# One convolution tap per channel group from TensorE to VectorE, six low parts of weights from VectorE to GpSimd

## The chip, the cores and the metric

The kernel runs on one core of a Trainium2 chip. The metric is the device time of one execution in microseconds; the value given is the median of the runs.

## What is computed

Two blocks of two layers each on a sequence of 256 tokens with 1024 features. The first layer of the first block is the one that matters here: a convolution mixer, then a layer norm, then a mixture of 16 experts, whose weights are the bulk of what is read from memory. The mixer, from the reference:

```python
def conv_mixer(x, w_in, a_dw, a_dw_b, a_ln_g, a_ln_b, b_dw, w_out):
    u = jnp.einsum("bsd,de->bse", x, w_in)
    a_val, a_gate, b_b, b_c, b_x = jnp.split(
        u, [D_A, 2 * D_A, 2 * D_A + D_B, 2 * D_A + 2 * D_B], axis=-1)
    a = a_val * jax.nn.sigmoid(a_gate)
    a = causal_depthwise_conv(a, a_dw) + a_dw_b
    a = jax.nn.silu(layer_norm(a, a_ln_g, a_ln_b))
    bb = b_b * causal_depthwise_conv(b_c * b_x, b_dw)
    return jnp.einsum("bse,ed->bsd", jnp.concatenate([a, bb], axis=-1), w_out)
```

## The kernel before

**Weights and their split.** All weights stream through slots of SBUF in a fixed order (`STREAM`, `LOAD_ORDER`), issued by SyncE in `sync_load`; a load waits until the earlier content of its slot is released (`released`), for a dense chunk when the low part of its fourth piece has been made. A dense chunk has 2048 columns, four pieces of 512. `even_w_in` (`ew_in`) has 10 chunks, pieces 0 to 39, and `even_w_out` (`ew_out`) 4 chunks, pieces 40 to 55. Each piece is multiplied in three products of two halves: ScalarE makes the high part `wh` (`scalar_split`, line 409), VectorE the low part `wl = w - wh` (`vector_split`, line 415), and in two other stages GpSimd makes the low parts of four pieces (`pool_split`, line 422). There are four places for parts, so piece p + 4 can be split when TensorE has used piece p (`w_used`). TensorE's three products are lines 444 to 446 (`three`). `low_made` names the semaphore that says a low part is there.

**The first mixer.** Each engine has its own hand-written order. `even_tensor` goes through chunks 1 to 9 of `ew_in` (`tensor_features`, 12 matmuls of 256 columns for each piece), then `ew_out` chunk 0, which multiplies `GT[0:2]`, the gated product of the short convolution, through its parts `early_gh` and `early_gl` (line 631). Then come the mean matmuls of the layer norm (line 1051), which need all four `ev_sum`, then the residual (line 1385), the next `ew_out` chunk, the variance (line 1060) and the rest.

**The 31 taps** act on four groups of 128 channels, each 256 tokens wide. The first `PE_TAPS` (9) of each group are matmuls with a diagonal matrix (line 1038), 36 in all, issued two behind each piece of chunks 3 to 6 and one behind each piece of chunk 7. ScalarE makes the diagonals (line 1100), six buffers in turn. Tap 9 is made by ScalarE (`ev_first_tap`, line 1094), and the other 21 per group by VectorE (`convolve`, line 1176), each adding to `acc`. A tap reads `aP` and `acc`, both in SBUF, and a column of weights. `steps` says how many taps VectorE makes behind each low part (4 where nothing is said, from chunk 3 on), and what else it does there: `value` (line 1167), `product` (1183), `convolve_b` (1190), `gate_b` (1197). What is left is made by `convolve(len(taps))` after the loop; then the four `ev_sum` (line 1219) add the matmuls' part from PSUM.

**ScalarE** goes in the same steps: the high part of the piece one chunk ahead, then up to two diagonals, then what else is due. **GpSimd** has one instruction in the mixer until its norm, the `pow` for the variance (line 1273).

Of the kernel before, what the change touches and what calls it, by code (L numbers as in the profile page):

```python
# [18 lines left out]
LN_EPS, RMS_EPS = 1e-5, 1e-6  # L19
RING, SMALL_RING, EXTRA = 12, 7, 12  # L20
PIECE, NPIECE = 512, 4
PE_TAPS = 9
MIXER_OUT = ("ew_out", "ow_out")
ROUTED = ("ew_out", "ow_out")
CH = 2048
# [21 lines left out]
CHUNK, KIND, PIECES, RUN_END = {}, [], {}, []  # L47
# [44 lines left out]
def f32(ap):  # L92
    return ap.bitcast(F32)
# [106 lines left out]
class Signals:  # L200
# [11 lines left out]
    def up(self, name, *step):  # L212
        shared = SHARED.get(name, name)
        steps = self.made.setdefault(shared, {})
        assert (name, *step) not in steps, (name, step)
        steps[(name, *step)] = len(steps) + 1
        return self.sem(shared), 1

    def at(self, name, *step):
        shared = SHARED.get(name, name)  # L220
        return self.sem(shared), self.known[shared][(name, *step)] if self.known else 1


class Kernel:
# [193 lines left out]
    def pool_split(self, p):  # L418

        pool = self.pool  # L420
        pool.wait_ge(self.at("w_hi", p))
        pool.e.tensor_tensor(self.wl[:, p % NPIECE, :], self.piece_source(p), f32(self.wh[:, p % NPIECE, :]),
                             ALU.subtract).then_inc(*self.up("w_lo_pool", p))

    def low_made(self, p):

        by_pool = any(0 <= p - PIECES[name] < NPIECE for name in ("ow_in", "aq0"))
        return self.at("w_lo_pool" if by_pool else "w_lo", p)

    def scalar_split_after(self, p):  # L430
# [1 line left out]
            self.scalar_split(p + NPIECE)  # L432

    def vector_split_after(self, p):
        if p + NPIECE < RUN_END[p]:
            self.vector_split(p + NPIECE)

    def weight(self, p):
# [573 lines left out]
    def even_tensor(self):  # L1012
        pe, at, up, PS, v = self.pe, self.at, self.up, self.PS, self.even_views()
        pe.wait_ge(at("consts", "ident"))
        for _ in range(7):
            pe.e.matmul(PS[:, 7, 0:128], self.ident[:, :], self.ident[:, :], start=True, stop=True)
        for q in range(4):
            pe.wait_ge(self.x_in[q // 2])
            for j in range(2):
                k = 2 * q + j  # L1020
                for h in range(2):
                    t = pe.e.transpose(PS[:, q, j * 256 + h * 128:j * 256 + h * 128 + 128],
                                       self.X[:, h, k * 128:k * 128 + 128], self.ident[:, :])
            t.then_inc(*up("turned", "ev", q))
            if q % 2:
                self.tensor_busy(7, 1)
        p, conv = PIECES["ew_in"], 0
        for c in range(10):
            if c == 0:
                self.tensor_opening_chunk("ev", p, 6)  # L1030
                continue
            if c >= 6:
                pe.wait_ge(self.even_bank_read((0, 1, 4, 5)[c - 6]))
            for _ in self.tensor_features("ev", p + 4 * c, (None, 1, 2, 3, 4, 5, 0, 1, 4, 5)[c]):
                for _ in range(0 if c < 3 or c > 7 else 1 if c == 7 else 2):
                    ch, k = conv // PE_TAPS, conv % PE_TAPS
                    pe.wait_ge(at("ev_dve", 1 + 2 * (ch // 2)), at("ev_diag", conv), at("ev_pad"))
                    pe.e.matmul(PS[:, 6 + ch // 2, ch % 2 * 256:ch % 2 * 256 + 256], v["dgs"][conv % 6],  # L1038
                                v["aP"][:, ch, k:k + 256], start=(k == 0), stop=(k == PE_TAPS - 1)).then_inc(
                        *up("ev_conv", conv))  # L1040
                    conv += 1
        assert conv == 4 * PE_TAPS
        p = PIECES["ew_out"]
        for c in (2, 3, 6, 7):
            pe.wait_ge(self.even_bank_read(c))
        for _ in self.tensor_out("ew_out", p, 8, 0):
            pass
        pe.wait_ge(at("consts", "mean"))
        for c in range(4):
            pe.wait_ge(at("ev_sum", 3))  # L1050
            t = pe.e.matmul(PS[:, 6, 0:256], self.mean512[:, :], v["acc"][:, c, :], start=(c == 0), stop=(c == 3))
        t.then_inc(*up("ev_mean"))
        for b in range(2):
            self.tensor_residual(b)
        for n in self.tensor_out("ew_out", p, 8, 1):
            if n == p + 4:
                pe.wait_ge(at("ev_square"))
                for h in range(2):
                    for c in range(4):
                        t = pe.e.matmul(PS[:, 7, h:h + 1], v["sq"][:, c, h * 128:h * 128 + 128], self.mean512[:, 0:1],  # L1060
                                        start=(c == 0), stop=(c == 3))
                t.then_inc(*up("ev_var"))
            if n == p + 5:
                pe.wait_ge(at("ev_rdiag", 1), at("consts", "ones"))
                for h in range(2):
                    t = pe.e.matmul(PS[:, 6, h * 128:h * 128 + 128], self.ones[:, 0:128], v["rs"][:, h * 128:h * 128 + 128],
                                    start=True, stop=True)
                t.then_inc(*up("ev_spread"))
        for b in range(2, 4):
            self.tensor_residual(b)  # L1070
        for _ in self.tensor_out("ew_out", p, 8, 2):
            pass
        self.tensor_out_last("ew_out", p, 8)

    def even_scalar(self):
# [11 lines left out]
        for c in range(10):  # L1087
            for j in range(4):
# [3 lines left out]
                for ch in {(2, 0): (0, 1), (4, 0): (2, 3)}.get((c, j), ()):  # L1092
                    act.wait_ge(at("ev_dve", 1 + 2 * (ch // 2)), at("ev_pad"))
                    act.e.activation(v["acc"][:, ch, :], v["aP"][:, ch, PE_TAPS:PE_TAPS + 256], ACT.Copy,
                                     scale=v["aw"][:, ch, PE_TAPS:PE_TAPS + 1]).then_inc(*up("ev_first_tap", ch))
                for _ in range(0 if c < 2 else 2 if diag < 4 * PE_TAPS - 1 else 4 * PE_TAPS - diag):
                    if diag >= 6:
# [171 lines left out]

    def even_pool(self):  # L1270
        pool, sm = self.pool, self.sm
        pool.wait_ge(self.at("var_eps", "ev"), self.at("consts", "mhalf"))
        pool.e.tensor_tensor(sm[:, 500:502], sm[:, 490:492], self.mhalf[:, 0:2], ALU.pow).then_inc(*self.up("rstd", "ev"))
        self.pool_norm("ew_out")
# [2062 lines left out]
```

## Time and profile before

| | us |
|---|---|
| median of 3 runs | 1743.29 |
| lowest, highest | 1742.96, 1743.67 |
| profiled execution | 1743.21 |
| its span | 1741.9 |
| TensorE busy | 1699.2 (98%) |
| VectorE busy | 793.8 (46%) |
| ScalarE busy | 623.6 (36%) |
| GpSimd busy | 126.0 (7%) |
| queue of the weight loads, share of the DMA engines | 77.2% |

The profiled execution lies 0.08 us under the median, and 1.3 us of it lie outside the span. The shares are averages over stages with different limits: in the two expert layers transfers and TensorE carry the time, in the dense stages TensorE with VectorE and ScalarE that make its operands. The granted TensorE clock is full (0.996 of 2.4 GHz). The first mixer takes the stretch from 0 to some 112 us; its convolution lies between 27 and 88 us.

### The profile page before, as it was taken

What the parts mean: (1) busy time and instruction counts of PE and PEld (TensorE: products, weight loads), DVE (VectorE), ACT (ScalarE), POOL (GpSimd) and SP (SyncE); (2) the same over time, 40 slices, a digit from 0 to 9 for tenths busy, and PEclk for the clock granted to TensorE, in tenths of its full rate; (3) what the DMA queues carried; (4) which work ended last, traced back from release to release, by engine and by line L of the source; (5) the groups of instructions that cost most, each with busy time, mean ns of one, the idle gap of its engine ahead of it and who ended that gap; (6) DMA issues with size and microseconds to landing.
All of it is one profiled execution on the core that took longest, in us unless ns stands there. A gap on an engine that the chain in (4) does not pass through costs nothing.

```text
span 1741.9 us, 23928 instructions
## 1 busy us (share of the span) xinstructions
PE 1699.2 (98%) x9970; PEld 1111.2 (64%) x9970; DVE 793.8 (46%) x1528; ACT 623.6 (36%) x1197; POOL 126.0 (7%) x150
## 2 busy tenths in 40 slices
PE   9999999998999999999999989999999999999998
PEld 9974334433234984344343333887999899789997
DVE  6961111111003791111111012866888677868885
ACT  6541100000003660100010002656666564756665
POOL 0000000000001000000000001231111011301101
PEclk9999999999899999999999999999999999999999
DMA  9869999999999799999999999534555544435550
GB/s 384 340 255 413 424 428 427 428 427 427 426 424 420 291 378 394 422 430 428 428 428 427 426 426 419 198 125 142 186 178 194 194 169 146 145 134 176 187 194 24
DMA packets 56948, 544.90 MB, mean 313 GB/s; under 512 B 6400, under 2 KB 6400, under 8 KB 8832
## 3 DMA queue, kind: packets, MB, share of 16 engines
q1 hardware_dynamic: 56416, 542.14, 77.2%
q8 instruction: 83, 1.36, 0.3%
q10 hardware_dynamic: 416, 1.13, 0.2%
q14 instruction: 33, 0.27, 0.0%
HBM read 542.19 MB, written 1.05 MB: 312 GB/s over the span
## 4 chain that ended last, share of the span: by engine, by line
PE 77%; DMA 17%; DVE 4%; issue 1%; ACT 1%; POOL 0%; ACTq 0%; SPq 0%; DVEq 0%
PE PS L1324 24%; DMA ring<-in_w 17%; PE PS L444 13%; PE PS L446 13%; PE PS L445 13%; PE PS L1306 2%; PE PS L1378 2%; PE PS L1524 2%; PE PS L1038 1%; PE PS L1340 1%; PE PS L2068 1%; PE PS L1392 1%; DVE wl L415 1%; PE PS L1497 1%; DVE sm L658 0%
## 5 line engine op out<-in xcount | busy, mean ns | idle before, releaser
L1324 PE MATMUL PS<-ring,F 128*64 128x512 f32 x1984 | 446.7, 598 | 23.7 <-DMA ring<-in_w 15.6
L415 DVE TENSOR_TENSOR wl<-ring,wh 128x512 fp32r<-128x512 f32 x496 | 359.4, 743 | 136.5 <-ACT wh L409 133.7
L409 ACT ACTIVATE wh<-ring 128x512 fp32r<-128x512 f32 x504 | 314.9, 630 | 266.5 <-PE PS L446 245.7
L1324 PEld LDWEIGHTS PS<-ring,F 128*64 128x64 f32 x1984 | 140.3, 137 | 306.8 <-issue 273.9
L444 PE MATMUL PS<-xh,wl 128*128 128x256 f32 x1120 | 322.3, 288 | 0.7 <-DVE wl L415 0.7
L445 PE MATMUL PS<-xl,wh 128*128 128x256 f32 x1120 | 316.8, 283 | 0.0
L446 PE MATMUL PS<-xh,wh 128*128 128x256 f32 x1120 | 316.8, 283 | 0.0
L444 PEld LDWEIGHTS PS<-xh,wl 128*128 128x128 f32 x1120 | 214.7, 192 | 3.7 <-DVE wl L415 2.0
L445 PEld LDWEIGHTS PS<-xl,wh 128*128 128x128 f32 x1120 | 214.8, 192 | 0.5
L446 PEld LDWEIGHTS PS<-xh,wh 128*128 128x128 f32 x1120 | 214.7, 192 | 0.0
L444 PE MATMUL PS<-wh,xl 128*128 128x512 f32 x320 | 129.7, 405 | 0.2 <-DVE F L2609 0.2
L1851 DVE COPY F<-PS 64x512 f32<-64x512 f32 x26 | 18.1, 695 | 223.1 <-PE PS L1324 223.1
L1826 DVE SCALAR_TENSOR_TENSOR F<-F,PS 128x512 f32<-128x512 f32 x28 | 19.3, 688 | 209.1 <-ACT F L1641 209.1
L446 PE MATMUL PS<-wh,xh 128*128 128x512 f32 x272 | 106.2, 391 | 0.0
L445 PE MATMUL PS<-wl,xh 128*128 128x512 f32 x272 | 106.1, 390 | 0.0
L1831 DVE SCALAR_TENSOR_TENSOR F<-F,PS 128x512 f32<-128x512 f32 x28 | 19.3, 688 | 172.7 <-PE PS L1324 172.7
L1324 PE MATMUL PS<-F 128*64 128x512 f32 x384 | 87.1, 593 | 0.0
L1641 ACT ACTIVATE F<-PS 128x512 f32<-128x512 f32 x28 | 16.7, 597 | 194.3 <-PE PS L1324 194.3
L1659 ACT ACTIVATE F<-PS 64x512 f32<-64x512 f32 x26 | 15.4, 591 | 187.6 <-PE PS L1324 187.6
L2801 DVE SCALAR_TENSOR_TENSOR F<-PS,cols,F 128x254 f32<-128x254 f32 (+1 forms) x176 | 76.4, 475 | 1.6
L1324 PE MATMUL PS<-early,F 128*64 128x512 f32 x336 | 76.1, 594 | 0.0
L1649 ACT ACTIVATE F<-PS 128x512 f32<-128x512 f32 x28 | 16.6, 595 | 152.5 <-PE PS L1392 152.5
(453 smaller groups left out, 2048.2 us busy)
## 6 DMA issues: line engine op xcount, KB each, us to landing
ring<-in_w SPq DMA_DIRECT2D x98, 2048.0 KB, 25.3
ring<-in_w SPq DMA_DIRECT2D x68, 1024.0 KB, 11.1
ring<-in_ffn_up SPq DMA_DIRECT2D x44, 1024.0 KB, 4.9
early<-in_w SPq DMA_DIRECT2D x16, 2048.0 KB, 26.2
F<-in_w SPq DMA_DIRECT2D x15, 2048.0 KB, 26.1
F<-in_w SPq DMA_DIRECT2D x22, 1024.0 KB, 10.5
ring<-in_ffn_down SPq DMA_DIRECT2D x22, 1024.0 KB, 4.9
ZX<-in_w SPq DMA_DIRECT2D x7, 2048.0 KB, 26.3
```

The lines of the kernel that those rows point to most:

```text
L409: act.e.activation(self.wh[:, p % NPIECE, :], self.piece_source(p), ACT.Copy).then_inc(*self.up("w_hi", p))
L415: dve.e.tensor_tensor(self.wl[:, p % NPIECE, :], self.piece_source(p), f32(self.wh[:, p % NPIECE, :]), ALU.subtract).then_inc(*self.up("w_ ...
L444: e.matmul(out, left[1], right[0], start=first, stop=False)
L445: e.matmul(out, left[0], right[1], start=False, stop=False)
L446: return e.matmul(out, left[0], right[0], start=False, stop=last)
L1306: t = pe.e.matmul(self.PS[:, 6 + half, k4 * 128:k4 * 128 + 128], self.X[:, h, k * 128:k * 128 + 128], v["S"][:, h, :], start=(h == 0), sto ...
L1324: t = pe.e.matmul(PS[64 * half:64 * half + 64, bank, :], lhs(k), weights[:, a:a + 512], start=(k == 0), stop=(k == 7))
L1378: t = pe.e.matmul(self.PS[:, b, :], v["Gt"][:, h, d, :], v["Y"][d], start=(q == 0), stop=False)
L1524: t = pe.e.matmul(PS[64 * half:64 * half + 64, self.first_bank(ex, 0), :], xg[:, k, ex * 64:ex * 64 + 64], weights[:, a:a + 512], start=(k ...
L1826: e.scalar_tensor_tensor(out=self.silu(ex), in0=self.silu(ex), scalar=1.0, in1=PS[:, 4, :], op0=ALU.add, op1=ALU.mult).then_inc(*up("silu" ...
L1831: e.scalar_tensor_tensor(out=v["hh"], in0=self.silu(ex), scalar=0.5, in1=PS[:, 5, :], op0=ALU.mult, op1=ALU.mult).then_inc(*up("hidden", l ...
L2801: t = dve.e.scalar_tensor_tensor(out=dst[:, j, s:256], in0=ps[:, j, 0:256 - s], scalar=cw[:, k, 2 - s:3 - s], in1=dst[:, j, s:256], op0=AL ...
```

## The change

`PE_TAPS` becomes 8. TensorE makes 32 conv matmuls, two behind each piece of chunks 3 to 6 and none in chunk 7. ScalarE makes 32 diagonals and tap 8 as the first one; VectorE makes taps 9 to 30, 22 per group, 88 in all instead of 84. The numbers in `steps` are as they were.

The low parts of the last piece of chunks 3 to 8 (pieces 15, 19, 23, 27, 31 and 35, `SHARED_LOWS`) are made by GpSimd, at the head of its part of the mixer. Each of these waits for its high part and for VectorE's low part of the piece before, so that the release of the slot, which follows this fourth low part, still says that all four were read. `low_made` sends TensorE's and SyncE's waits for these pieces to GpSimd's semaphore.

```diff
-PE_TAPS = 9
+PE_TAPS = 8
@@ pool_split
         pool.wait_ge(self.at("w_hi", p))
+        if p in self.SHARED_LOWS:
+            pool.wait_ge(self.at("w_lo", p - 1))
         pool.e.tensor_tensor(self.wl[:, p % NPIECE, :], self.piece_source(p), f32(self.wh[:, p % NPIECE, :]),
                              ALU.subtract).then_inc(*self.up("w_lo_pool", p))

+    SHARED_LOWS = [PIECES["ew_in"] + 4 * c + 3 for c in range(3, 9)]
+
     def low_made(self, p):
-        by_pool = any(0 <= p - PIECES[name] < NPIECE for name in ("ow_in", "aq0"))
+        by_pool = p in self.SHARED_LOWS or any(0 <= p - PIECES[name] < NPIECE for name in ("ow_in", "aq0"))
@@ vector_split_after
-        if p + NPIECE < RUN_END[p]:
+        if p + NPIECE < RUN_END[p] and p + NPIECE not in self.SHARED_LOWS:
             self.vector_split(p + NPIECE)
@@ even_tensor
-                for _ in range(0 if c < 3 or c > 7 else 1 if c == 7 else 2):
+                for _ in range(0 if c < 3 or c > 6 else 2):
@@ even_pool
         pool, sm = self.pool, self.sm
+        for p in self.SHARED_LOWS:
+            self.pool_split(p)
```

## Rows read from the trace of the kernel before

**Rows 1.** Busy time by stretches: stretch, its length, busy us by engine, clock, DMA

```profile
50.00:60.00 10.00, 10.00 (x73) 9.56 (x72) 9.97 (x23) 5.74 (x13) 0.00 (x0) 1.00 1.01 424
60.00:70.00 10.00, 10.00 (x75) 9.62 (x74) 9.98 (x24) 5.02 (x10) 0.00 (x0) 1.00 1.03 424
70.00:80.00 10.00, 10.00 (x84) 9.95 (x83) 10.00 (x21) 5.28 (x10) 0.00 (x0) 1.00 0.58 215
120.00:130.00 10.00, 9.61 (x56) 6.03 (x55) 3.40 (x21) 2.21 (x6) 0.00 (x0) 1.00 0.57 200
```

**Rows 2.** Chain that ended last, first mixer: start, length, what

```profile
70.20 0.43 PE PS L1038 x2
...
82.15 0.24 issue
82.39 0.47 PE PS L444
82.86 0.23 PE PS L445
...
88.11 1.73 PE PS L1051 x8
```

**Rows 3.** Timeline of VectorE, first mixer: start, length, line, instruction

```profile
44.21 1.67 DVE L1176 SCALAR_TENSOR_TENSOR F<-F,cols 128x256 f32<-128x256 f32 x4
45.89 0.69 DVE L415 TENSOR_TENSOR wl<-ring,wh 128x512 fp32r<-128x512 f32 x1
...
48.66 0.69 DVE L415 TENSOR_TENSOR wl<-ring,wh 128x512 fp32r<-128x512 f32 x1 [0.49 <-ACT wh L409]
...
53.64 1.67 DVE L1176 SCALAR_TENSOR_TENSOR F<-F,cols 128x256 f32<-128x256 f32 x4
55.22 0.69 DVE L415 TENSOR_TENSOR wl<-ring,wh 128x512 fp32r<-128x512 f32 x1
55.82 0.88 DVE L1176 SCALAR_TENSOR_TENSOR F<-F,cols 128x256 f32<-128x256 f32 x2
...
57.32 0.69 DVE L415 TENSOR_TENSOR wl<-ring,wh 128x512 fp32r<-128x512 f32 x1
...
59.61 0.69 DVE L415 TENSOR_TENSOR wl<-ring,wh 128x512 fp32r<-128x512 f32 x1
...
61.90 0.69 DVE L415 TENSOR_TENSOR wl<-ring,wh 128x512 fp32r<-128x512 f32 x1
...
81.41 0.70 DVE L631 TENSOR_TENSOR early_gl<-F,early_gh 128x512 fp32r<-128x512 f32 x1
...
85.00 0.89 DVE L1176 SCALAR_TENSOR_TENSOR F<-F,cols 128x256 f32<-128x256 f32 x2
85.79 1.66 DVE L1219 SCALAR_TENSOR_TENSOR F<-F,sm,PS 128x256 f32<-128x256 f32 x4
```

**Rows 4.** Timeline of ScalarE, high parts of pieces 28, 29 and 30

```profile
56.68 0.61 ACT L409 ACTIVATE wh<-ring 128x512 fp32r<-128x512 f32 x1
58.22 0.83 ACT L1100 ACTIVATE F<-ident,cols 128x128 f32<-128x128 f32 x2 [0.93 <-PE PS L1038]
58.96 0.62 ACT L409 ACTIVATE wh<-ring 128x512 fp32r<-128x512 f32 x1
...
61.25 0.61 ACT L409 ACTIVATE wh<-ring 128x512 fp32r<-128x512 f32 x1
```

**Rows 5.** Timelines of GpSimd and VectorE in a later dense stage, side by side

```profile
1223.85 1.61 POOL L2845 TENSOR_TENSOR F<-F 128x512 f32<-128x512 f32 x1
...
1234.66 1.29 POOL L2845 TENSOR_TENSOR F<-F 128x512 f32<-128x512 f32 x1
...
1234.77 1.73 DVE L415 TENSOR_TENSOR wl<-ring,wh 128x512 fp32r<-128x512 f32 x1 [0.68 <-ACT wh L409]
```

**Rows 6.** Timelines of GpSimd and VectorE after the first expert layer

```profile
550.43 1.28 POOL L422 TENSOR_TENSOR wl<-ring,wh 128x512 fp32r<-128x512 f32 x1 [435.79 <-ACT wh L409]
...
550.24 2.00 DVE L658 BATCH_NORM_STATS2 sm<-PS 128x6 f32<-128x512 f32 x3
```

## The prediction

> **What bounds the kernel now.** I read the busy time by stretches first. From 50 to 80 us both TensorE and VectorE are full (10.00 and 9.97 to 10.00 of 10), and the DMA share falls from 1.03 to 0.58: the weight slots are filled and the transfers wait for slots [rows 1]. So the first mixer is a compute stage, and what it ends late by moves the expert layer behind it; after 120 us the transfers start again with the slots that the experts give back (share 0.57 from 120 to 130, most of it idle time) [rows 1]. Second, the chain of waits: through the stretch it is TensorE alone, one matmul behind the other. It breaks once, at 82.15, where the first `ew_out` matmul waits for a low part of `GT` that VectorE ended at 82.11; that matmul ends at 82.86, while its followers end 0.23 apart [rows 2]. The mean matmuls (`ev_mean`) take 88.11 to 89.84, and TensorE has no gap before them [rows 2]. They need the last `ev_sum`. Third, VectorE's own timeline: the four `ev_sum` instructions start at 85.79 and last 1.66, so they end at 87.45, only 0.66 us before TensorE reaches them [rows 3]. Both engines are nearly critical at the point where they meet. The question is which of them the change helps, and the views to answer it are the timelines of VectorE and ScalarE and the rows where GpSimd and VectorE already run together.
>
> **TensorE.** Four conv matmuls of 36 go, one per channel group: all four single ones of chunk 7. The chain has such a single one at 0.43 [rows 2]; the four save 4 x 0.43 = 1.72 us, between 64 and 71 us. TensorE would stand before the mean at 88.11 - 1.72 = 86.4 if nothing else held it. ScalarE loses four `ev_diag` instructions (two take 0.83 [rows 4]) that no one waits for; its splits of pieces 29 and 30 no longer stand behind the diagonals, and come sooner.
>
> **VectorE, without contention.** It gains four taps. `convolve` takes a fixed number per step, so all four land in the last `convolve(len(taps))`, straight before the sums: two taps there now last from 85.00 to 85.79 [rows 3], so one costs 0.395 and four cost 1.58. It loses the low parts of pieces 15, 19, 23, 27, 31 and 35 (one is 0.60 from start to next start: 55.22 to 55.82 [rows 3]). Three of them save nothing: up to piece 24 VectorE waits for ScalarE (0.49 before 48.66, the low part of piece 24, and 0.1 a step before that: four taps and the low part after them are 1.68 apart at 44.21 and 45.89, where undelayed ones are 1.58 apart at 53.64 and 55.22 [rows 3]), and TensorE's and so ScalarE's pace is unchanged there. Piece 27 saves nothing either: piece 28's low part starts at 57.32, when its high part lands (56.68 + 0.61 = 57.29 [rows 3, 4]). What pays is 31 and 35: 2 x 0.60 = 1.20, and two waits of 0.10 for ScalarE, at 59.61 and 61.90, each right behind a high part (58.96 + 0.62, 61.25 + 0.61 [rows 3, 4]), where ScalarE will be earlier. Sum: +1.58 - 1.20 - 0.20 = +0.18: the sums end at 87.45 + 0.18 = 87.63, after TensorE's 86.4 and its earlier low part of `GT`. So even in the kind case the 1.72 us of TensorE is spent waiting for the sums. The mean starts at 87.7 from a standstill; a restart costs 0.25 to 0.5 (the first matmul after the gap at 82.15 took 0.24 + 0.47 where 0.23 is the pace [rows 2]), so the mean ends at 87.7 + 0.3 + 1.73 = 89.7 against 89.84. Gain: 0.1 us.
>
> **GpSimd.** Six subtracts are added. GpSimd has the same instruction on the same shape in later stages: 1.28 us [rows 6]. It is idle in this stretch, and TensorE wants each result about two pieces later. The tightest is piece 35: TensorE runs chunks 8 and 9 from 70.63 to 82.15, 1.44 a piece [rows 2], so it wants piece 35 at 70.63 + 3 x 1.44 - 1.72 = 73.2. Piece 34's low part, by the lag worked out below, ends near 71.3 and GpSimd's near 72.6. Nothing is late there. Its wait for the low part of p - 1 only keeps the slot release honest; SP, which issues the weight loads in order, gets the slots of these six chunks up to 0.6 later (1.28 - 0.69), and the loads behind one wait with it; while transfers queue anyway (share 1.01 and more to 70 us [rows 1]) and the slots are full before the experts start, that costs nothing; without that cover it would be 0.6.
>
> But the two engines disturb each other. A VectorE low part that starts at 1234.77 takes 1.73 instead of 0.69 while GpSimd's two-input TENSOR_TENSOR (1234.66, 1.29) runs: it ends 0.55 after GpSimd does [rows 5]. The loss is 1.04 us for 1.18 us of overlap: VectorE practically stands still. GpSimd in turn takes 1.61 instead of 1.29 when VectorE was there first [rows 5]. Instructions that read PSUM are spared: three statistics of PSUM beside the very subtract that is moved here take 2.00 us, 0.67 each, no more than the 0.69 of one undisturbed VectorE instruction over 512 elements (the low part at 55.22) [rows 3, 6]. In the mixer nearly all VectorE work reads two SBUF operands: low parts (`ring`, `wh`) and taps (`aP`, `acc`). No row shows a tap beside GpSimd. Its cost is bounded by zero (as the PSUM readers) and by GpSimd's whole 1.28; I take the low part's behaviour as nearest, 1.04 plus a little because VectorE is back to back here and never begins 0.11 late: 1.15 a piece. So each moved low part saves 0.60 and costs 1.15: +0.55, not -0.60. The Trainium skill, "SBUF — State Buffer", section "Who interferes with whom", states the general form: a VectorE instruction with two SBUF inputs and a GpSimd one that reads SBUF exclude each other for the whole instruction, whatever the operation. By it the taps are held like the low parts, and each piece costs the full 1.28, which adds 0.4 us to the sum below.
>
> **The sum.** VectorE's lag against before: pieces 15 to 23 cost 0.55 each, and VectorE has 0.8 us of waiting a chunk to take that in (three steps of 0.1 and the 0.49 [rows 3]): 0. Piece 27: +0.55 less the 0.1 that it waits before 57.32: +0.45. The waits at 59.61 and 61.90: -0.20. Pieces 31 and 35: +1.10. So the low part of `GT` comes at 82.11 + 1.35 = 83.46 and `ew_out` starts 1.35 late, though TensorE was 1.72 early. The four taps: +1.58. The last sum ends at 87.45 + 2.93 = 90.38. TensorE, ready at 88.11 + 1.35 = 89.46, waits 0.9; the mean ends at 90.38 + 0.3 + 1.73 = 92.4, 2.6 us later than 89.84. Behind it TensorE is the chain again and everything moves by the same 2.6 us; the experts' first slots are released by TensorE, so the stream restarts 2.6 later too. Span 1741.9 + 2.6 = 1744.5; the profiled execution's time 1743.21 + 2.6 = 1745.8; it lies 0.08 under the median of the runs, 1743.29, so the median becomes 1745.9. That is +0.15%. A measurement of this kernel can tell 0.2%, which is 3.5 us, from no change; this stays inside.
>
> **Rivals.** (A) GpSimd doesn't hold the taps, because a SCALAR_TENSOR_TENSOR is spared: then the sum without contention holds, -0.1: 1743.2. For: not all that VectorE does is held [rows 6], and no row has a tap beside GpSimd. Against: [rows 5], with two SBUF operands as the taps have. (B) The exclusion is dearer: each subtract first waits for the running VectorE instruction, is stretched to 1.61 as in [rows 5], and VectorE stands for all of it. Then a piece costs 1.61 - 0.60 = 1.01; 27, 31 and 35 give 0.91 + 2.02 - 0.20 = 2.73, with the taps 4.31, and some 0.3 that pieces 15 to 23 no longer hide; the mean ends 4.3 us late: 1747.6, slower by 0.25%. It decides when a piece costs more than about 1.45. Against: in [rows 5] the stretch came from a wait during which VectorE worked, so it is not lost twice. (C) TensorE's saving survives whole, since VectorE catches up: -1.7, 1741.6. It would need VectorE's sums 1.0 us earlier than now, and no row gives it that. (D) The loss is taken in behind the mixer, by a transfer wait that ends last: 1743.3. Against: slots are full before 120 us [rows 1], and no transfer is awaited there.
>
> **Chances.** Forecast 0.68; A 0.12, B 0.14, C 0.02, D 0.04. Own range of the forecast, from 1.04 to 1.28 a piece and restart 0.25 to 0.5: 1745.3 to 1746.7. For 8 in 10, with A or B partly: 1742.9 to 1747.3. Faster by over 0.2% would need 3.5 us, twice what TensorE sheds: 0.01. Slower by over 0.2%: B and a sliver of the forecast, 0.15. Within: 0.84.
>
> **What would show it.** Taps or low parts of 1.4 to 1.7 us at pieces 15 to 35, each ending just behind a GpSimd subtract; conv matmuls gone after 64.5; the last taps ending near 88.8 and the sums near 90.4; TensorE idle up to 1 us before the mean, naming VectorE's sum. If taps stay at 0.5 (0.89 less 0.395) beside GpSimd, A is right. If TensorE has no gap before the mean, my account of the last taps is wrong. If the mean comes 2.6 late and the span doesn't, D.

## The result, and the profile after

The changed kernel takes 1745.53 us (median of 22 runs, 1743.94 to 1748.35) against 1743.16 for the kernel before (22 runs, 1742.46 to 1745.30) beside it. The ratio is 1.0015, with a 95% interval of 1.0009 to 1.0021: slower by 2.4 us, and by less than the 0.2% taken as the bound of no change. The profiled execution took 1745.91, its span 1744.7.

The busy time of the changed kernel by stretches (columns as in [rows 1]) shows VectorE full from 60 to 90 us, while TensorE is not from 70 us on. Before, it was the other way round from 80 to 90 us: TensorE 9.76 of 10, VectorE 9.38.

```profile
60.00:70.00 10.00, 10.00 (x80) 9.72 (x79) 10.00 (x22) 4.91 (x9) 4.24 (x1) 1.00 1.01 419
70.00:80.00 10.00, 9.66 (x80) 9.35 (x79) 10.00 (x20) 4.52 (x9) 1.41 (x1) 1.00 0.53 202
80.00:90.00 10.00, 7.16 (x36) 5.69 (x35) 10.00 (x22) 4.80 (x8) 0.00 (x0) 1.00 0.69 255
```

The chain of the changed kernel, where [rows 2] had TensorE with one break of 0.24 us, runs through VectorE's taps, low parts and sums into the mean matmuls:

```profile
65.31 0.60 DVE wl L415
65.91 2.23 DVE F L1180 x3
...
83.46 0.86 DVE F L1180 x2
84.33 0.60 DVE wl L415
84.93 0.60 DVE F L1201
...
87.91 1.58 DVE F L1223 x4
89.49 0.14 issue
89.62 1.96 PE PS L1055 x8
```

The reader is to see the 2.23 for three taps, which otherwise take 1.19, and at the end that the mean matmuls (line 1055) wait for the sums (line 1223) and then take 1.96 instead of 1.73. The view of waits of TensorE from 60 to 100 us names the low part of `GT`, the sums and once, for 0.3 us, a low part of VectorE. It never names GpSimd, and from 20 to 60 us TensorE has no wait, so no low part that moved came too late for it:

```profile
PE PS L448 <- DVE early_gl L635: 1.7, 1, 1.7
PE PS L1055 <- DVE F L1223: 1.1, 1, 1.1
PE PS L448 <- DVE wl L415: 0.3, 1, 0.3
```

GpSimd's timeline in the mixer has the six added subtracts, for pieces 15, 19, 23, 27, 31 and 35:

```profile
27.08 1.32 POOL L424 TENSOR_TENSOR wl<-ring,wh 128x512 fp32r<-128x512 f32 x1 [22.48 <-ACT wh L409]
36.53 2.18 POOL L424 TENSOR_TENSOR wl<-ring,wh 128x512 fp32r<-128x512 f32 x1 [8.13 <-ACT wh L409]
45.69 1.47 POOL L424 TENSOR_TENSOR wl<-ring,wh 128x512 fp32r<-128x512 f32 x1 [6.98 <-ACT wh L409]
54.83 2.17 POOL L424 TENSOR_TENSOR wl<-ring,wh 128x512 fp32r<-128x512 f32 x1 [7.68 <-ACT wh L409]
62.83 4.24 POOL L424 TENSOR_TENSOR wl<-ring,wh 128x512 fp32r<-128x512 f32 x1 [5.83 <-ACT wh L409]
70.68 1.41 POOL L424 TENSOR_TENSOR wl<-ring,wh 128x512 fp32r<-128x512 f32 x1 [3.61 <-DVE wl L415]
```

VectorE's timeline beside them, as [rows 3]:

```profile
27.18 2.29 DVE L1180 SCALAR_TENSOR_TENSOR F<-F,cols 128x256 f32<-128x256 f32 x3
...
43.96 4.27 DVE L1180 SCALAR_TENSOR_TENSOR F<-F,cols 128x256 f32<-128x256 f32 x8
...
53.39 2.45 DVE L1180 SCALAR_TENSOR_TENSOR F<-F,cols 128x256 f32<-128x256 f32 x6
55.76 0.68 DVE L1187 TENSOR_TENSOR F<-F,PS 128x512 f32<-128x512 f32 x1
57.08 0.69 DVE L415 TENSOR_TENSOR wl<-ring,wh 128x512 fp32r<-128x512 f32 x1 [0.64 <-ACT wh L409]
...
65.83 2.31 DVE L1180 SCALAR_TENSOR_TENSOR F<-F,cols 128x256 f32<-128x256 f32 x3
...
70.46 2.70 DVE L1180 SCALAR_TENSOR_TENSOR F<-F,cols 128x256 f32<-128x256 f32 x4
...
85.46 2.45 DVE L1180 SCALAR_TENSOR_TENSOR F<-F,cols 128x256 f32<-128x256 f32 x6
87.84 1.64 DVE L1223 SCALAR_TENSOR_TENSOR F<-F,sm,PS 128x256 f32<-128x256 f32 x4
```

Four taps without a neighbour last 1.66 from the first's start to the last's end, three 1.27. The groups at 27.18, 43.96, 65.83 and 70.46 are each longer by 1.02 to 1.04. The six taps at 53.39 are not, though GpSimd's subtract starts at 54.83 in their midst; it takes 2.17 instead of 1.28, so it waits for about 0.9 us, until VectorE comes to `product`, which reads PSUM (55.76). Piece 19's subtract does the same with `value`, which reads PSUM too: 36.53 + 2.18 - 1.28 = 37.43, and `value` starts at 37.46.

**One mark for all traces.** The first conv matmuls come between 27.3 and 28.7 us in the traces here, whatever the kernel; so I lay the traces on the start of the first pair of conv matmuls and count from there. In TensorE's timeline of the kernel before it is

```profile
27.86 1.02 PE L1038 MATMUL PS<-F 128*128 128x256 f32 x4
```

and in the changed kernel's

```profile
27.61 1.02 PE L1042 MATMUL PS<-F 128*128 128x256 f32 x4
```

From this mark, in us. "Sums" are the four `ev_sum` instructions; the names in the first column are those of the runs in the next section; the last column runs from the first matmul of the first expert (line 1524 in the kernel before) to GpSimd's first low part behind that expert layer (an expectation below calls it the stretch from the first gather):

| kernel | sums end | against before | mean matmuls end | against before | length of the first expert layer |
|---|---|---|---|---|---|
| before | 59.59 | | 61.98 | | 425.65 |
| changed | 61.87 | +2.28 | 63.97 | +1.99 | 426.64 |
| changed, again | 61.85 | +2.26 | 63.97 | +1.99 | 425.51 |
| taps_only | 60.97 | +1.38 | 63.09 | +1.11 | 426.58 |
| lows_only | 60.51 | +0.92 | 62.88 | +0.90 | 426.10 |
| extra_subtract | 63.45 | +3.86 | 65.79 | +3.81 | 425.37 |
| extra_memset | 59.59 | 0.00 | 61.98 | 0.00 | 425.73 |
| late_two | 61.85 | +2.26 | 63.96 | +1.98 | 425.69 |
| two_free_lows | 60.98 | +1.39 | 63.08 | +1.10 | 425.13 |
| balanced | 59.40 | -0.19 | 61.52 | -0.46 | 426.50 |
| balanced_nine | 58.83 | -0.76 | 61.56 | -0.42 | 425.37 |
| nudge_short | 61.85 | +2.26 | 63.97 | +1.99 | 425.42 |
| nudge_long | 61.86 | +2.27 | 63.98 | +2.00 | 425.84 |

The mixer's columns repeat to 0.02 us between executions (the two traces of the changed kernel); the last column doesn't. So the mixer is read from the traces, and the run times only confirm it.

### The profile page after: what moved, and what is told of

Same layout as the page of the kernel before. It is cut to its first block, busy times and chain, and to the rows that moved or that the text cites. A ratio compares the mean times of both kernels' runs of the same rounds, so it can differ in the third digit from the quotient of the medians.

```text
span 1744.7 us, 23918 instructions
## 1 busy us (share of the span) xinstructions
PE 1696.0 (97%) x9962; PEld 1109.3 (64%) x9962; DVE 795.4 (46%) x1526; ACT 622.1 (36%) x1193; POOL 138.9 (8%) x156
## 4 chain that ended last, share of the span: by engine, by line
PE 75%; DMA 18%; DVE 5%; issue 1%; ACT 1%; POOL 0%; ACTq 0%; SPq 0%; DVEq 0%
PE PS L1330 23%; DMA ring<-in_w 17%; PE PS L448 13%; PE PS L450 12%; PE PS L449 12%; PE PS L1312 2%; PE PS L1384 2%; PE PS L1530 2%; DMA ring<-in_a_w_in 1%; DVE wl L415 1%; DVE F L1180 1%; PE PS L2074 1%; PE PS L1042 1%; PE PS L1398 1%; PE PS L1503 1%
## 5 line engine op out<-in xcount | busy, mean ns | idle before, releaser
L415 DVE TENSOR_TENSOR wl<-ring,wh 128x512 fp32r<-128x512 f32 x490 | 354.9, 742 | 137.6 <-ACT wh L409 135.1
```

Of the source, the lines that this page charges most:

```text
L415: dve.e.tensor_tensor(self.wl[:, p % NPIECE, :], self.piece_source(p), f32(self.wh[:, p % NPIECE, :]), ALU.subtract).then_inc(*self.up("w_ ...
```

## The experiments

**Each half of the change alone.** The taps:

```diff
-    SHARED_LOWS = [PIECES["ew_in"] + 4 * c + 3 for c in range(3, 9)]
+    SHARED_LOWS = []
```

> The changed kernel with all low parts of the mixer back on VectorE: only the move of one tap per channel group is left. My theory (VectorE sets the end of the convolution, and the four taps land straight before its sums): VectorE's sums end 1.58 - 0.20 = 1.4 us later than before (88.8), TensorE stands idle before the mean matmuls about 0.9 us, their end comes at 90.9 instead of 89.84, and the time rises by 1.1 us. Rival (TensorE sets it, its four matmuls less pay): the mean matmuls end 1.7 us earlier and the time falls by 1.7 us.

Measured: the sums 1.38 later, the mean matmuls 1.11; TensorE's wait before them is 1.1 us. The time is 1744.70 against 1743.37 (ratio 1.0009, 1.0000 to 1.0018). VectorE's timeline and the chain of this kernel:

```profile
84.73 2.46 DVE L1180 SCALAR_TENSOR_TENSOR F<-F,cols 128x256 f32<-128x256 f32 x6
87.11 1.64 DVE L1223 SCALAR_TENSOR_TENSOR F<-F,sm,PS 128x256 f32<-128x256 f32 x4
...
88.77 0.14 issue
88.90 1.97 PE PS L1055 x8
```

Six taps stand before the sums where [rows 3] had two. TensorE's four matmuls less bring nothing: the rival, 1.7 us earlier, falls.

The low parts, on the changed kernel:

```diff
-PE_TAPS = 8
+PE_TAPS = 9
@@ even_tensor
-                for _ in range(0 if c < 3 or c > 6 else 2):
+                for _ in range(0 if c < 3 or c > 7 else 1 if c == 7 else 2):
```

> The kernel before with the six low parts on GpSimd and nothing else changed. My theory (a GpSimd subtract stops VectorE's instructions with two SBUF operands for 1.04 us, more than the 0.60 that the moved low part saves, and only pieces 31 and 35 count, since VectorE waits for ScalarE up to piece 28): VectorE's sums and the mean matmuls come 2 x 0.44 = 0.9 us later, the time rises by 0.9 us; up to 1.3 if piece 27 counts too. Rival (no exclusion): VectorE's sums come 1.2 us earlier, TensorE is the bound as before, the wait of 0.24 to 0.5 us at the start of the output product goes, and the time falls by 0.2 to 0.5 us.

Measured: sums +0.92, mean matmuls +0.90, time 1744.73 against 1743.37 (1.0007, 0.9998 to 1.0016). Taking six low parts of 0.60 off VectorE makes it later. The rival, a gain, falls. The two halves add up to the whole: 1.38 + 0.92 = 2.30 for the sums, where the changed kernel has 2.28. But TensorE meets the delay at another place here: it has no wait before the mean matmuls and one of 1.1 us (0.2 in the kernel before) at the low part of `GT`, which ends 0.91 later.

**What excludes what.** The kernel before with GpSimd work that no one needs:

```diff
@@ even_pool, on the kernel before
+        free = self.F[:, 6272:6528]
+        wide = [free.bitcast(mybir.dt.bfloat16).rearrange("p (a b) -> p a b", a=2)] + [x.unsqueeze(1).to_broadcast([128, 2, 256]) for x in (self.cmask[:, :], self.ones[:, :])]
+        for p in [PIECES["ew_in"] + 4 * c + 3 for c in range(3, 9)]:
+            pool.wait_ge(self.at("consts", "cmask"), self.at("w_hi", p), self.at("w_lo", p - 1))
+            pool.e.tensor_tensor(wide[0], wide[1], wide[2], ALU.subtract).then_inc(*self.up("consts", "extra", p))
+            pool.wait_ge(self.at("consts", "extra", p))
```

> The kernel before, with six GpSimd subtracts added beside it at the same six places (they read two idle tiles of 512 elements a partition and write a third; no one waits for them); VectorE keeps all its low parts and TensorE its 36 taps. My theory (exclusion, about 1.04 us for each that meets two-operand VectorE work): pieces 31 and 35 cost 2.1, 27 up to 0.9, and each of the first three leaves up to 0.3 that the waits for ScalarE don't take in: VectorE's sums and the time come 2.1 to 3.5 us later. Rival (the two engines run side by side freely): no difference, since nothing waits for these instructions.

Measured: sums +3.86, time 1747.07 against 1743.37 (1.0024, 1.0014 to 1.0034). VectorE's timeline at pieces 27 and 31:

```profile
54.98 2.69 DVE L1176 SCALAR_TENSOR_TENSOR F<-F,cols 128x256 f32<-128x256 f32 x4
...
64.55 2.69 DVE L1176 SCALAR_TENSOR_TENSOR F<-F,cols 128x256 f32<-128x256 f32 x4
```

The direction and the price of one are as expected (2.69 is 1.03 over 1.66), the sum is 0.4 above the range. Piece 28's low part already starts 2.0 us late, counted from the mark (31.47 against 29.46); two waits of 0.1 take 0.2 of it, and pieces 31 and 35 add 2.07. I had let the waits for ScalarE take in too much of the first four. One of them is piece 27, whose subtract met taps here, and not an instruction that reads PSUM (2.69 at 54.98).

```diff
@@ in place of the subtract
+            for i in range(4):
+                pool.e.memset(free, 0.0).then_inc(*self.up("consts", "extra", p, i))
+                pool.wait_ge(self.at("consts", "extra", p, i))
```

> As the run with the added subtracts, but each is replaced by four GpSimd memsets of 256 elements (about 1.2 us together) that read nothing. My theory (what excludes is the reading of SBUF): VectorE's instructions keep 0.48 and 0.69 us beside them, the mean matmuls end where they did, the time stays within 0.3 us. Rival (any GpSimd work on SBUF stops VectorE): the same loss as with the subtracts, 2.1 us or more.

Measured: sums and mean matmuls to the hundredth where they were; 1743.16 against 1743.37 (1.0001, 0.9992 to 1.0011). GpSimd's and VectorE's timelines at piece 31:

```profile
63.05 1.42 POOL L1276 MEMSET F<- 128x256 f32 x4 [6.77 <-ACT wh L409]
...
62.26 1.67 DVE L1176 SCALAR_TENSOR_TENSOR F<-F,cols 128x256 f32<-128x256 f32 x4
```

The same time of GpSimd work, writing only, leaves the taps at 1.67. GpSimd's writing is thereby ruled out as what stops VectorE, and its reading is what is left. The memsets differ from the subtract in more than that: they are another operation, and four short instructions in place of a long one. No run separates these. This is how the Trainium skill has it ("SBUF — State Buffer", "Who interferes with whom"): a VectorE instruction with two SBUF inputs contends with a GpSimd instruction that reads SBUF and not with one that only writes.

**Which of the six count.** Two kernels, with the changed kernel's list cut:

```diff
-    SHARED_LOWS = [PIECES["ew_in"] + 4 * c + 3 for c in range(3, 9)]
+    SHARED_LOWS = [PIECES["ew_in"] + 4 * c + 3 for c in (7, 8)]
```

> The changed kernel with only pieces 31 and 35 on GpSimd; 15, 19, 23 and 27 go back to VectorE. My theory (the first four cost and save nothing, since VectorE waits for ScalarE up to piece 28 in either case): VectorE's sums and the mean matmuls stand where they stand in the changed kernel, 2.3 and 2.0 us behind the kernel before when both traces are laid on their first conv matmul; the time within 0.3 us of the changed kernel's. Rival (each of the six costs the same): a third of the loss from GpSimd, 2 x 0.44 of the sums' 2.3, has to be spread over six, and the sums come 0.6 us earlier than in the changed kernel.

```diff
+    SHARED_LOWS = [PIECES["ew_in"] + 4 * c + 3 for c in (4, 6)]
```

> The changed kernel with only pieces 19 and 27 on GpSimd, the two whose subtract gets its turn beside a VectorE instruction that reads PSUM. My theory: no VectorE instruction is stretched, the sums and the mean stand as with the taps alone (1.38 and 1.1 us behind the kernel before on the same mark), for VectorE gives the time that it saves back as a wait for ScalarE. Rival (exclusion costs at any place): 0.9 us more than that.

Measured: with 31 and 35 alone the sums stand at +2.26, as with all six; with 19 and 27 alone at +1.39, as with none. Both as expected. The times are 1744.32 against 1743.05 (1.0007, 0.9998 to 1.0016) and, one run, 1743.02, where the mixer's +1.1 drowns in the scatter.

**The taps elsewhere.** `balanced` is the changed kernel with all low parts on VectorE, `balanced_nine` the kernel before; in both, `steps` becomes (shortened):

```diff
-                 (2, 3): [(convolve, 2)], (3, 3): [(convolve, 2), (value, 1)], ...
-                 (7, 0): [(convolve, 3)], (7, 1): [(convolve, 3)], (7, 2): [(convolve, 3)],
+                 (2, 3): [(convolve, 4)], (4, 1): [(convolve, 5)], (4, 3): [(convolve, 5)], (3, 3): [(convolve, 2), (value, 1)], ...
+                 (7, 0): [(convolve, 2)], (7, 1): [(convolve, 2)], (7, 2): [(convolve, 2)],
```

> PE_TAPS 8, all low parts on VectorE, and the taps' places changed: two more behind piece 15's low part and one more each behind those of 21 and 23, where VectorE waits for ScalarE, and one less behind each of 32, 33 and 34, so three fewer stand before the low part of GT. My theory: the sums end 1.38 - 4 x 0.395 = 0.2 us earlier than before, the low part of GT 1.4 us earlier, so output product 1.4 us earlier; the mean matmuls end at the sums' 87.25 + 0.14 + 1.96 = 89.35, 0.5 us earlier than before; the time falls by 0.5 us, too little to be told by the time alone. Rival (TensorE's four matmuls are what counts once VectorE is not in the way): 1.7 us.

> The kernel before (PE_TAPS 9, nothing on GpSimd) with the taps' places changed in the same way. My theory: VectorE's sums come 1.6 us earlier, but TensorE is then the one that ends last; only its wait for the low part of GT goes, and the mean matmuls end 0.5 us earlier (0.24 + 0.24); the time falls by 0.5 us. Rival (VectorE alone sets the end in the kernel before too): 1.6 us earlier.

Measured, `balanced`: sums -0.19, mean matmuls -0.46, as expected (-0.2, -0.5), so its rival, 1.7 us earlier, falls; 1742.53 against 1743.05 (0.9998, 0.9989 to 1.0007). `balanced_nine`: mean matmuls -0.42 as expected, but the sums only -0.76 instead of -1.6; 1742.92 against 1743.05 (1.0001, 0.9992 to 1.0010). VectorE's timeline of `balanced_nine` shows why, at pieces 35 and 36:

```profile
71.21 0.69 DVE L415 TENSOR_TENSOR wl<-ring,wh 128x512 fp32r<-128x512 f32 x1 [0.36 <-ACT wh L409]
...
73.14 0.69 DVE L415 TENSOR_TENSOR wl<-ring,wh 128x512 fp32r<-128x512 f32 x1 [0.24 <-ACT wh L409]
```

VectorE, freed of three taps just before, waits for ScalarE again, which follows TensorE, and TensorE still has its four matmuls in chunk 7. Piece 35's low part should have come 1.19 earlier (three taps) and comes 0.74 earlier, piece 36's 0.40 earlier: these two waits cost the missing 0.8. Both versions put the mixer some 0.45 us ahead of the kernel before; neither beats it by a time that can be told.

**How GpSimd gets in.** Piece 31's subtract took 4.24 us, of which 1.28 are its own; `late_two` gave 4.24 once more, `lows_only` 1.30. I took it for a matter of phase and shifted the request by a memset of 16 or 160 elements:

```diff
@@ pool_split, on late_two
             pool.wait_ge(self.at("w_lo", p - 1))
+            pool.e.memset(self.F[:, 6272:6288], 0.0).then_inc(*self.up("consts", "nudge", p))
+            pool.wait_ge(self.at("consts", "nudge", p))
```

> The changed kernel with only pieces 31 and 35 on GpSimd, and a memset of 16 elements before each of the two subtracts, which shifts them by about 0.15 us. My theory (when GpSimd asks for the port against back-to-back VectorE work, the phase decides whether it is let in at once or waits for many instructions; VectorE loses its 1.04 us once in either case): piece 31's subtract takes 1.3 to 1.5 us instead of 4.24, and the sums stay where they are, 2.3 us behind the kernel before. Rival (a kind of VectorE instruction or the piece decides): 4.24 again.

> The same with memsets of 160 elements, a shift of about 0.3 us. My theory: the phase decides again, so that one of the two subtracts may wait long (over 2 us) or both be let in at once; the sums again 2.3 us behind the kernel before, within 0.3. Rival (the piece decides): 4.24 for piece 31 and 1.4 for piece 35 again.

GpSimd's timelines, the short shift first:

```profile
63.70 4.07 POOL L426 TENSOR_TENSOR wl<-ring,wh 128x512 fp32r<-128x512 f32 x1
...
71.54 1.64 POOL L426 TENSOR_TENSOR wl<-ring,wh 128x512 fp32r<-128x512 f32 x1
```

```profile
63.28 3.95 POOL L426 TENSOR_TENSOR wl<-ring,wh 128x512 fp32r<-128x512 f32 x1
...
71.12 1.52 POOL L426 TENSOR_TENSOR wl<-ring,wh 128x512 fp32r<-128x512 f32 x1
```

The theory of the phase falls: the subtract starts later and ends at the same place in VectorE's sequence, behind piece 32's low part, so 4.24 becomes 4.07 and 3.95. Counted from the mark it ends between 39.45 and 39.47 in the changed kernel's two traces, `late_two`, `nudge_short` and `nudge_long`. The sums didn't move. The piece alone doesn't decide either, for `lows_only` has 1.30 at piece 31. What lets GpSimd in stays open.

**The changed kernel again.**

> The changed kernel again, for a second trace of it. My theory (the mixer's loss is fixed by the orders of the engines, and what its first trace showed beyond it, 1.0 us more in the first expert layer, is that execution's own): on the mark of the first conv matmul the sums come 2.3 and the mean matmuls' end 2.0 us after those of the kernel before, and the stretch from the first gather to the end of the first expert layer is anywhere between 425.1 and 426.6 us. Rival (the change makes the first expert layer slower too): that stretch is again 426.6 or more.

Measured: sums +2.26 and mean matmuls +1.99, and 425.5 us for the expert layer where the first trace had 426.6. The time is 1745.35 against 1743.62 (1.0010, 1.0001 to 1.0019). The extra 1.0 us in the first trace was that execution's own: over all thirteen traces this stretch lies between 425.1 and 426.6 without regard to the mixer.

## Why the prediction was right, point by point

- **What bounds.** Right: VectorE's last sum sets the mean matmuls (TensorE waits 1.1 us for it, 0.9 forecast), and the 1.72 us that TensorE sheds go nowhere. `taps_only` puts the sums at +1.38, which is 1.58 - 0.20 to the hundredth.
- **Where the four taps land.** Right: six taps last 2.45 before the sums at 87.84, where two did in [rows 3].
- **The price of a moved low part.** The mechanism was right, taps are held like low parts (rival A falls with `lows_only` and with the 2.31 and 2.70 above). The size was a little off: 1.04 for each, exactly the loss in [rows 5], not 1.15. VectorE's back-to-back work does not make it dearer, and 1.28, the price for a hold over GpSimd's whole instruction, was too high as well. So +0.44 a piece instead of +0.55. B (1.61 lost) falls too: GpSimd's own time grows to 4.24, yet VectorE loses 1.04.
- **Which pieces count.** One term was wrong: piece 27 was put at +0.45 and costs nothing. Its subtract got in with `product`, which reads PSUM, and ended in VectorE's wait of 0.64 before 57.08; in `extra_subtract`, where the same piece met taps, they took 2.69 in place of 1.66. I had not looked at what VectorE would be doing when GpSimd is let in.
- **The sum.** Forecast +2.93 for the sums, measured +2.28. The difference is piece 27's 0.45 and 2 x 0.11 for the price: 2.26 is left, which is what `late_two` and the second trace of the changed kernel show. The same two terms explain the low part of `GT`: +1.35 forecast, +0.67 measured (54.92 against 54.25 from the mark). The mean matmuls: +2.6 forecast, +2.0 measured. So the mechanism came as forecast, and the delay was put 0.6 us too long.
- **The restart.** 0.3 was forecast over 1.73; measured are 0.14 of issue and 1.96, together 0.37.
- **GpSimd's results.** "Nothing is late there" held for TensorE, but not for the reason given: piece 31's low part was there 2.5 us later than VectorE's used to be (39.46 against 36.93 from the mark), where up to 0.6 was reckoned. Its slot is released by so much later too; the DMA share from 60 to 70 us stays at 1.01 (1.03 before).
- **Behind the mixer.** The first matmul of the first expert comes at 96.92 from the mark in the kernel before and 98.93 in the changed one, +2.01: the loss is handed on whole, D falls. The loads move with it: the group issued at 126.75 in the kernel before is issued at 128.51 in the changed one, +2.01 from the mark. One reading was wrong and did no harm: the transfers don't start again after 120 us; in the kernel before their share is 1.01 from 110 to 120 already. That the median (1745.53, +2.4) came as near to the forecast (1745.9, +2.6) as it did owes something to luck: the traces support +2.0, which over 1743.16 is 1745.2, just under the forecast's own range (1745.3 to 1746.7), and the repeated comparison gave +1.7.
- **C** falls with `taps_only`: TensorE's saving doesn't survive.

## What to carry to other kernels

Before work goes from VectorE to GpSimd, look in the trace for a place where both run: if VectorE's instruction reads two operands from SBUF and GpSimd's reads two as well, the stretched instruction gives the price of the move. Here it was 1.04 us for each subtract of 1.28, against 0.60 saved, so the move lost 0.44 wherever VectorE had no wait to take it in. Where GpSimd got in beside a VectorE instruction that reads PSUM (pieces 19 and 27), the move cost nothing; it gained nothing either, because VectorE waited for ScalarE there. Work taken from one of two engines that meet gains nothing if the other has no slack (1.72 us off TensorE gave nothing here), and with hand-written orders where the work lands matters as much as its amount: here added taps fell straight before the result that all wait for, while the waits they could have filled lay 30 us and more before.

## What the runs showed of the hardware that I had not expected

- GpSimd can wait for its turn through many VectorE instructions. In the changed kernel its subtract for piece 31 starts at 62.83 and, by its own 1.28, was let in near 65.8 (an estimate): it waited through six taps of the long and the short convolution and a low part, back to back. In `lows_only`, at the same point of the taps (0.76 us after the group's start, against 0.77), it was let in at once. The shifts of 0.2 and 0.3 us did not change the place. VectorE loses its 1.04 us once, wherever in back-to-back taps it is let in.
- The loss is the same for a low part of 512 elements ([rows 5]) and for a tap of 256: 1.02 to 1.06 us for a GpSimd instruction of 1.28 (the most in `lows_only`, 2.73 for four taps that take 1.67).
- After a wait of about 1.1 us TensorE's eight mean matmuls take 1.96 in the chain instead of 1.73, at the full granted clock, and they start 0.14 after VectorE's end. Most of the 0.23 is no slower work: in the timeline, which counts from the first one's start, they take 1.96 and in the kernel before 1.89, of which 0.16 overlap the matmul before them. The other 0.07 is one matmul of 454 ns, where the longest before takes 382. In `balanced`, after a wait of 0.7, the eight take 1.97.
